# Router products of a two-layer decoder trunk: the turned residual as the stationary operand, and the last turned copy ahead of the square

## What is computed

```python
def moe_swiglu(h, router_w, wg, wu, wd):
    logits = (h @ router_w).astype(jnp.float32)
    top_val, top_idx = lax.top_k(logits, TOP_K)
    top_w = jax.nn.softmax(top_val, axis=-1)
    gates = jnp.sum(jax.nn.one_hot(top_idx, N_EXPERTS, dtype=jnp.float32) * top_w[..., None], axis=-2).astype(h.dtype)
    y = jnp.zeros_like(h)
    for e in range(N_EXPERTS):
        y = y + gates[..., e:e + 1] * swiglu(h, wg[e], wu[e], wd[e])
    return y
...
        h = rms_norm(x, ffn_norm_g[layer])
...
            x = x + moe_swiglu(h, router_w[j], expert_w_gate[j], expert_w_up[j], expert_w_down[j])
```

## Time and profile before

| | us |
|---|---|
| median of 3 executions | 1379.6 |
| lowest and highest | 1379.42, 1381.24 |
| the profiled execution | 1380.94 |
| its span from the first to the last instruction | 1379.1 |
| PE busy | 1367.3 |
| DVE busy | 807.1 |
| ACT busy | 661.2 |
| router, from the last adding to `x` to the gather (in the trace) | 584 to 591 |

### The profile page before, as it was taken

One profiled execution on the slowest core, in us unless ns is written; L12 is line 12 of the kernel. 1 busy time (PEld: TensorE's weight loads), 2 busy tenths in 40 slices (PEclk: granted clock), 3 DMA queues, 4 the chain that ended last, 5 costly groups with the idle time before them and its releaser, 6 DMA issues.

```text
span 1379.1 us, 17450 instructions
## 1 busy us (share of the span) xinstructions
PE 1367.3 (99%) x6662; PEld 936.9 (68%) x6662; DVE 807.1 (59%) x1142; ACT 661.2 (48%) x885; POOL 7.3 (1%) x16
## 2 busy tenths in 40 slices
PE   8999999999999999999999999999999999999998
PEld 7887788888898877843434778534878534778532
DVE  5878665555567786632113889423989423989311
ACT  7657646444466575511002787302787302787210
POOL 1000000000000000000000000000000000000000
PEclk9999999999999999999999999999999999999999
DMA  9655446555544567899999999999999999999997
GB/s 353 219 179 183 153 130 238 183 183 183 183 148 158 184 246 271 314 401 428 429 430 429 430 430 428 428 431 429 430 430 427 429 429 429 430 431 428 422 430 301
DMA packets 84308, 455.88 MB, mean 331 GB/s; under 512 B 5424, under 2 KB 7728, under 8 KB 58112
## 3 DMA queue, kind: packets, MB, share of 16 engines
q1 hardware_dynamic: 83376, 453.20, 81.9%
q0 software_dynamic: 560, 1.28, 0.4%
q10 hardware_dynamic: 288, 0.27, 0.1%
HBM read 453.68 MB, written 1.05 MB: 330 GB/s over the span
## 4 chain that ended last, share of the span: by engine, by line
PE 91%; DVE 3%; ACT 3%; DMA 3%; issue 0%; SPq 0%; DVEq 0%; ACTq 0%
PE pA L850 39%; PE pB L850 19%; PE pB L1355 10%; PE pA L1355 8%; PE pA L1419 7%; PE pA L874 2%; DMA first_run<-expert_w_gate_dram 2%; PE pB L874 1%; DVE w_lo L1884 1%; PE pB L1253 1%; ACT w_hi L1520 1%; DMA raw<-w_in_dram 1%; PE pA L1283 0%; PE pB L1075 0%; ACT early_hi L1520 0%
## 5 line engine op out<-in xcount | busy, mean ns | idle before, releaser
L1884 DVE TENSOR_TENSOR w_lo<-raw,w_hi 128x1024 fp32r<-128x1024 f32 x127 | 151.8, 1220 | 60.6 <-ACT w_hi L1520 60.2
L1884 DVE TENSOR_TENSOR w_lo<-first_run,w_hi 128x1024 fp32r<-128x1024 f32 x126 | 148.8, 1218 | 28.4 <-ACT w_hi L1520 27.1
L1520 ACT ACTIVATE w_hi<-raw 128x1024 fp32r<-128x1024 f32 x127 | 130.9, 1058 | 58.3 <-PE pB L850 32.2
L1884 DVE TENSOR_TENSOR w_lo<-late,w_hi 128x1024 fp32r<-128x1024 f32 x126 | 150.6, 1222 | 12.7 <-ACT w_hi L1520 5.0
L1520 ACT ACTIVATE w_hi<-first_run 128x1024 fp32r<-128x1024 f32 x126 | 130.7, 1064 | 49.3 <-DMA first_run<-expert_w_gate_dram 25.7
L1520 ACT ACTIVATE w_hi<-late 128x1024 fp32r<-128x1024 f32 x126 | 131.6, 1059 | 31.3 <-PE pA L850 14.4
L1833 ACT ACTIVATE ex_act<-pA 64x512 f32<-64x512 f32 x15 | 8.9, 590 | 242.2 <-PE pA L1355 194.6
L1884 DVE TENSOR_TENSOR early_lo<-raw,early_hi 128x1024 fp32r<-128x1024 f32 x58 | 69.8, 1221 | 36.3 <-ACT early_hi L1520 36.2
L2394 DVE TENSOR_TENSOR x<-pA,x 128x512 f32<-128x512 f32 x28 | 18.8, 687 | 117.9 <-PE pA L1284 117.0
L1355 PE MATMUL pB<-late,x_narrow 128*64 128x512 f32 x272 | 78.0, 592 | 0.0
L850 PE MATMUL pA<-w_hi,hT_hi 128*128 128x512 f32 x192 | 77.1, 402 | 0.0
(11 more groups left out here) (457 smaller groups left out, 2789.5 us busy)
## 6 DMA issues: line engine op xcount, KB each, us to landing
first_run<-expert_w_gate_dram SPq DMA_DIRECT2D x28, 1792.0 KB, 19.1
first_run<-expert_w_up_dram SPq DMA_DIRECT2D x28, 1792.0 KB, 16.3
late<-expert_w_gate_dram SPq DMA_DIRECT2D x28, 1792.0 KB, 16.0
late<-expert_w_up_dram SPq DMA_DIRECT2D x28, 1792.0 KB, 17.8
raw<-w_in_dram SPq DMA_DIRECT2D x43, 1024.0 KB, 5.0
first_run<-expert_w_down_dram SPq DMA_DIRECT2D x21, 2048.0 KB, 16.8
late<-expert_w_down_dram SPq DMA_DIRECT2D x28, 1024.0 KB, 18.2
late<-expert_w_down_dram SPq DMA_DIRECT2D x14, 2048.0 KB, 21.5
```

The source lines that it names most:

```text
L1520: f(like_raw(m, halves_slot(m)[0]), raw_slot(m), ACT.Copy).then_inc(s["w_hi_done"], 1)
L1884: tt(like_raw(m, lo), raw_slot(m), like_raw(m, hi.bitcast(F32)), ALU.subtract).then_inc(s["w_lo_done"], 1)
```

## The change

The operands of the router products change places: the turned residual (128 channels by 128 tokens) is the stationary operand, and the 8 columns of router weights move. All sixteen products add into one place of bank B7 for each block of tokens, as tokens by logits, so there are no partial sums; `parts_sb`, `fold`, the two fold products and DVE's two copies go. `logit_psum` is told by the last product. On ACT the copy of the last 256 columns stands ahead of the square of block 1. On DVE the reciprocal stands behind the copy of the logits.

```diff
--- before.py
+++ after.py
@@ -313,8 +313,6 @@
             c0 = KT + S * k if k else 0
             return slice(c0, c0 + S * n)
         router = civ[:, 832:832 + KT * 32].rearrange("p (k n) -> p k n", k=KT)
-        fold = civ[:, 1088:1088 + NE]
-        parts_sb = civ[:, 576:576 + S]
 
         pairs = civ[:, 256:256 + 2 * A * NE * NE].rearrange("p (a e n) -> p a e n", a=A, e=NE)
         lower = civ[:, 512:512 + NE * NE].rearrange("p (e n) -> p e n", e=NE)
@@ -1102,10 +1100,9 @@
 
                     for i in range(4):
                         k = 4 * half + i
-                        ins = mm((B6, B5)[a][32 * i:32 * (i + 1), 0:P], router[:, k, :], xT[:, a, P * k:P * (k + 1)],
-                                 start=(half == 0), stop=True, skip_group_check=True)
-                    if half:
-                        ins.then_inc(s["narrow_psum"], 1)
+                        ins = mm(B7[:, NE * a:NE * (a + 1)], xT[:, a, P * k:P * (k + 1)], router[:, k, 0:NE],
+                                 start=(half, a, i) == (0, 0, 0), stop=True, skip_group_check=True)
+                    return ins
 
                 def turn_y(half):
                     pe.wait_ge(s["y_ready"], 2 * layer + half + 1)
@@ -1154,12 +1151,7 @@
                     route(1, 0)
                     pe.wait_ge(s["xb_act"], 4)
                     pe.wait_ge(s["xb_dve"], 1)
-                    route(1, 1)
-                    for a in range(A):
-                        pe.wait_ge(s["narrow_rows"], NL + a + 1)
-                        ins = mm(B7[:, NE * a:NE * (a + 1)], parts_sb[:, P * a:P * (a + 1)], fold, start=(a == 0),
-                                 stop=True, skip_group_check=True)
-                    ins.then_inc(s["logit_psum"], 1)
+                    route(1, 1).then_inc(s["logit_psum"], 1)
 
             mixer(0)
 
@@ -1772,10 +1764,11 @@
                 eng.wait_ge(s["xb_psum"], a + 1)
                 f(xT[:, a, 0:512], pA[:, 2 + a, :], ACT.Copy).then_inc(s["xb_act"], 1)
             split_to(EX0 + AHEAD - 1)
+            rms_block(0)
             for a, n in ((0, 512), (1, 256)):
-                rms_block(a)
                 eng.wait_ge(s["xb_psum"], A + a + 1)
                 f(xT[:, a, 512:512 + n], pA[:, a, 0:n], ACT.Copy).then_inc(s["xb_act"], 1)
+            rms_block(1)
             eng.wait_ge(s["rstd_ready"], 4)
             for a in range(A):
                 f(xn_v[:, a, :], x[:, a, :], ACT.Copy, scale=RSTD[:, a:a + 1]).then_inc(s["xn_ready"], 1)
@@ -1930,7 +1923,6 @@
                 eng.wait_ge(s["gate_psum"], 2)
                 gain = vec[:, R_FFNG + KT:R_FFNG + 2 * KT].unsqueeze(2).broadcast_to([P, KT, NE])
                 link(nc.vector.memset(router, 0.0))
-                nc.vector.tensor_reduce(fold, ident.rearrange("p (g c) -> p c g", g=4)[:, 0:NE, :], AX, ALU.add)
                 tt(router[:, :, 0:NE], wg_raw[:], gain, ALU.mult).then_inc(s["router_ready"], 1)
                 iota_n = cst[:, IOTA:IOTA + 1, 0:NE].broadcast_to([P, NE, NE])
                 iota_e = cst[:, IOTA, 0:NE].unsqueeze(2).broadcast_to([P, NE, NE])
@@ -2217,11 +2209,6 @@
 
             eng.wait_ge(s["xb_psum"], 2 * A)
             nc.vector.tensor_copy(xT[:, 1, 768:], B4[:, 0:256]).then_inc(s["xb_dve"], 1)
-            eng.wait_ge(s["rms_ready"], 8)
-            nc.vector.reciprocal(RSTD, RMS).then_inc(s["rstd_ready"], 1)
-            for a in range(A):
-                eng.wait_ge(s["narrow_psum"], NL + a + 1)
-                nc.vector.tensor_copy(parts_sb[:, P * a:P * (a + 1)], (B6, B5)[a][:, 0:P]).then_inc(s["narrow_rows"], 1)
             lg = sm(8, 16).rearrange("p (a e) -> p a e", a=A)
             t1, hot1, hot2 = [sm(c, 16).rearrange("p (a e) -> p a e", a=A) for c in (24, 40, 56)]
             m1, m2, idx = sm(72, A), sm(74, A), sm(76, A)
@@ -2231,6 +2218,8 @@
 
             eng.wait_ge(s["logit_psum"], 1)
             link(nc.vector.tensor_copy(lg, bank_as(B7, A, NE)))
+            eng.wait_ge(s["rms_ready"], 8)
+            nc.vector.reciprocal(RSTD, RMS).then_inc(s["rstd_ready"], 1)
             others = lg.unsqueeze(2).broadcast_to([P, A, NE, NE])
             own = lg.unsqueeze(3).broadcast_to([P, A, NE, NE])
             link(tt(pairs[:, :, :, NE:], others, own, ALU.is_equal))
```

## The result

| | before | after |
|---|---|---|
| median of 20 executions, us | 1380.28 | 1382.44 |
| lowest and highest | 1379.42, 1382.00 | 1380.43, 1390.24 |
| span of the profiled execution | 1379.1 | 1381.7 |

What follows compares the result with a forecast made beforehand. PE and the DMA weight stream were taken to run at nearly the same rate, the data having fallen 0.70 us behind. The end moves by max(0.45, 0.9 - 0.70) = +0.45 us from 1379.6 to 1380.0 us, range 1378.8 to 1382.0.

Steps and rivals of the forecast that it cites:

- A pass: Router products on PE: one full-width load with 8 moving columns was taken to cost 0.111 us, bounds 0.02 to 0.115.
- ScalarE's moved copy: Last copy ahead of the square on ScalarE: worth nothing, since PE is busy with its loads until it needs it.
- The cover of `xn`: ScalarE's scaled copies, moved later, end at about 591.1 us, before the gather at 592.0: the cover holds by 0.9 us.
- p: PE's delay on reaching the gather behind the router: 0.8 to 1.1 us, taken as 0.9.
- d: Time the DMA stream loses at the late `low_slots` request, where the queue can run dry: 0.1 to 0.8 us, taken as 0.45.
- the clock rival: Router stretch with little but loads lowers PE's granted clock, costing 1.7 us of work; end at 1381.7 us; chance 0.07.
- added to p it makes 2.6, to d 2.15: Sum for a clock fall of 1.7 us at the router: the end moves by max(2.15, 1.9), to 1381.7 us.
- Behind it each next unit is issued before the one ahead has landed, so the loss isn't paid twice: DMA queue after the `low_slots` request: later units lose nothing more, so the stream's loss stays at 0.45 us.
- the 0.45 of the sum: Forecast move of the kernel's end, the larger of the stream's loss 0.45 and PE's delay less slack 0.20: +0.45 us.
- 0.70 us of slack: PE's total wait for loads by the last wide job: delays of PE before 1169 us cost nothing up to 0.70 us.
- Nothing: Rival: passes cost about 0.06 us, logits come 0.5 us early, the stream stays full, end unmoved at 1379.6 us; chance 0.13.
- All of it gets through: Rival: queue empty at the `low_slots` request, so the stream shifts by PE's whole delay: +1.0, 1380.6 us; chance 0.15.

Runs made afterwards that it cites:

- copy_only: Kernel before with its own products and fold, but ScalarE's last copy ahead of the square and the reciprocal behind the logits copy; 1380.73 us, ratio 1.0001.
- products_only: Changed kernel without the move on ScalarE and with DVE's reciprocal in its old place; 1382.26 us, ratio 1.0018 against before.
- after_third: The changed kernel unaltered, third set of 12 executions, its profiled execution at low clock; 1387.06 us, ratio 1.0034 against before.
- busy_twice: Changed kernel with each router product made once more into unread columns, 128 columns moving in each; 1385.09 us, ratio 1.0027 against before.
- quiet_twice: Changed kernel with each router product made once more into unread columns, 8 columns moving in each; 1394.62 us, ratio 1.0083 against before.
- after_again: The changed kernel unaltered, second set of 12 executions; 1382.16 us, ratio 1.0018 against before.
- moving_128: Changed kernel with the 8 router columns repeated sixteen times as moving operand, only the first 8 read; 1381.01 us, ratio 1.0010 against before.
- moving_32: Changed kernel moving all 32 columns of the stored router block, 24 of them zero and unread; 1382.29 us, ratio 1.0012 against before.
- delay_1: Kernel before with one more unread product of 512 columns on PE ahead of the gather; 1380.48 us, ratio 1.0001.
- late_low: Kernel before with SP waiting for one more of PE's expert products before issuing the `low_slots` load; 1380.81 us, ratio 0.9997.

## Why the prediction missed

Of the 2.4 us between 1380.0 and 1382.44, 0.7 is the base: the forecast stood on the median of three executions of the kernel before, 1379.6, and that of twenty is 1380.28. The other 1.7 is the effect, +0.45 forecast and +2.16 measured.

**Right, by its own steps.** A pass costs 0.112 us (taken: 0.111). The logits are read 0.70 us later and the gather comes 0.77 us later (forecast 0.80 to 0.97 and 0.9); the little that was too much lies at the start, where the first loads came at 584.19, ahead of the 584.25 to 584.42 given, and the turning at 585.00, 0.16 us late and not 0.30 to 0.47. ScalarE's moved copy is worth nothing (copy_only, products_only). The cover of `xn` is 591.87 - 590.96 = 0.9 us, as forecast. The end follows the stream and not PE's own delay: p less 0.70 is 0.07, and the end moved by 2.5 with the data. And `low_slots` is where the queue is nearly empty: before, it landed after 5.9 us, and with the queue certainly empty it landed after 4.9 (after_third), 5.1 (busy_twice) and 5.4 us (quiet_twice), so there were 0.5 to 1.0 us in hand. In the first profile after it landed after 5.4, 0.82 - 0.5 = 0.3 us later than before, within the bounds of d at this place (0.1 to 0.8). In after_again, moving_128, products_only and moving_32 it landed after 5.0, between 0.2 us earlier and 0.1 us later than before: there this place passed on nothing.

**Wrong, the clock rival.** Its mechanism was the right one, its price and its chance were not. The price was taken from the fall at 16 to 20 us, 1.7 us of work. There the clock was below 1.00 in three windows of 2 us (0.97, 0.50 and 0.68). Here it stayed at half for 17 us, over products of up to 512 columns, and PE at half speed freed its buffers late, so the stream ran empty for 7.5 us. The step that failed is "added to p it makes 2.6, to d 2.15": with the measured numbers it is a request 8.6 us late and an end 8.9 us late. The chance was put at 0.07 on the ground that the gather, with 64 columns behind each load, keeps the full clock; that row was the wrong neighbour for 8 columns. It happened in 15 of 44 executions, and in 4 of 12 of products_only. With 128 columns moving behind the same loads it happened in 0 of 20 (moving_128, busy_twice); at a rate of 19 in 56, none in 20 would have a chance of 0.0003. The rate differs between the sets, so the firmer comparison is the one within a set: 0 of 9 for busy_twice beside 7 of 12 and 5 of 6. The Trainium skill (TensorE: Matmul & The Clock Gate, Part 1) has the clock go down after idle time of the array; the fall here came in a stretch in which the profile shows PE without idle time, a case that the page doesn't treat: it doesn't say whether weight loads count as work. The prediction said that by this rule the rival was likelier, and still gave it 0.07.

**Wrong, the size of d.** "Behind it each next unit is issued before the one ahead has landed, so the loss isn't paid twice" is the second step that failed. Without a fall, the data of the last wide job were late by 2.5, 1.05, 0.55 and 1.4 us (after, after_again, products_only, moving_32), and by 2.6 in moving_128, against the 0.45 of the sum. There is a second thin place, where the first pair of jobs begins, that I had not looked for. The request and its time to landing there, first before, then after:

```profile
678.28 0.33 SPq L726 DMA_DIRECT2D first_run<-expert_w_gate_dram  x1
...
first_run<-expert_w_gate_dram SPq DMA_DIRECT2D x1, 1792.0 KB, 8.8
```

```profile
679.05 0.33 SPq L724 DMA_DIRECT2D first_run<-expert_w_gate_dram  x1
...
first_run<-expert_w_gate_dram SPq DMA_DIRECT2D x1, 1792.0 KB, 8.9
```

From `once_parts` this request is 0.8 us late and its unit lands 0.9 us late, though the units ahead of it landed as before (0.1 us earlier). A request that is late by its full 0.8 us and takes no shorter to land had nothing in hand. The same unit landed 1.1 us late in after_again, 1.6 in moving_128, 0.8 in delay_1 and 4.6 in busy_twice; in products_only and moving_32 it landed only 0.3 us late, so the place is not equally thin in every execution. In after_again the 1.1 us stay almost unchanged up to the last wide job (1.05). The 0.70 us of slack that the sum took off p didn't help either: in delay_1 PE came 0.69 us late and the last narrow job 0.86, because the data had moved by 0.8 too.

**Open.** The first profile loses 1.5 us more at the request of 694.34, which landed after 16.4 us against 14.8 before, although the queue was full. This isn't the work of a late PE: copy_only, whose requests are early, makes a step of 0.9 us at the same request (from 0.6 us earlier than before to 0.3 later), moving_32 makes one of 1.1, and after_again and delay_1 make none. So how much of the 2.5 us belongs to the change and how much to the execution is open.

The ordinary executions' time is better told like with like. The early fall of the clock in the kernel before is a matter of the execution too: the profiles of delay_1, late_low and moving_32 don't have it, as these windows of delay_1 show (columns as in rows 9), nor do those of after_third and quiet_twice, which fell at the router.

```profile
16.00:18.00 2.00, 2.00 (x20) 1.72 (x18) 1.00 (x2) 1.73 (x4) 0.00 (x0) 1.00 1.03 393
18.00:20.00 2.00, 2.00 (x19) 2.00 (x18) 0.17 (x1) 1.06 (x3) 0.00 (x0) 1.00 1.08 416
```

Of the 85 executions of before, 45 have a mean clock of 0.999 or more and a median of 1380.2 us, and 40 have 0.997 or 0.998 and 1381.4. Of the 29 ordinary ones of the changed kernel, 5 are in the first group, at 1381.1, and 24 in the second, at 1382.2. Within each group the difference is 0.8 to 0.9 us: about PE's delay p, passed on in full, and twice the 0.45 of the sum. The bare medians of the ordinary ones, 1.9, 1.7 and 0.65 us above before in the three sets, 0.4 in products_only, 0.5 in moving_32 and 0.6 in moving_128, mix the two groups in different shares. This grouping was made after the fact and pools sets, so it is an estimate, not a test; why so few ordinary executions of the changed kernel are in the first group is open.

**The rivals that fell.** "Nothing" needed passes of 0.06 us; they cost 0.112. "All of it gets through" (chance 0.15) is what a long delay does (busy_twice), and by the estimate of 0.8 to 0.9 us nearly what an ordinary execution does, though by the second thin place and not by the first.

No version here is faster than the kernel before. The best form of the changed products is moving_128, 0.64 us slower by the medians and 1.4 by the ratio (0.1 to 2.5).

## What to carry to other kernels

Turning a small product round so that few columns move does not make it cheap: the full-width load sets its price, and here it also brought TensorE's clock down in 15 of 44 executions. When such a stretch can't be avoided, moving more columns than are needed behind the same loads cost 0.14 us here, and the clock stayed up in 20 of 20. Price a fall of the clock by what waits for the engine afterwards, buffers and their next transfers above all, and look for every place where the transfer queue is thin, not the first alone.

## What the runs showed of the hardware

- The clock fell in a stretch in which the profile shows PE busy for all of the time: 584 to 588 us in the low execution after_third, 2.00 of 2.00 us in both windows, with a clock of 1.00 and then 0.75. Once down, it stayed down through work that keeps the full clock when it is there already: the same unread products and gather run at 1.00 in the ordinary execution.
- The fall is a matter of the execution, not of the program alone: 15 of 44 with the same program, at 6 of 20, 2 of 12 and 7 of 12 in the three sets. A few executions alone would have shown either of two kernels, 1382 or 1388 us.
- At half clock a full-width load costs double as well: quiet_twice has two of them in 0.30 us before the fall and in 0.55 us after it.

The last point in the trace of quiet_twice, two rows of its timeline:

```profile
587.55 0.30 PEld L1103 LDWEIGHTS pB<-conv_in,ga 128*128 128x128 f32 x2
...
588.14 0.55 PEld L1103 LDWEIGHTS pB<-conv_in,ga 128*128 128x128 f32 x2
```

- One megabyte into a queue that was certainly empty landed after 4.9, 5.1 and 5.4 us (after_third, busy_twice, quiet_twice); what a queue has "in hand" is counted from there, with this scatter.
